# Last block's second network: rows scaled at eviction, queries and keys as rows, eleven tile places, paired scores, end in halves

## The reference

```
x   = rmsnorm(h, final_norm_w)                     # end of the first network
h   = rmsnorm(x, norm_g_2)
q, k, v, z_a, u_b, v_b, z_b, g_a, g_b = split(h @ w_in_2)   # 7 x 512, 2 x 1024 columns
y_a = stick_breaking(q, k, v) * silu(z_a)          # 8 heads of 64, causal
y_b = spatial_gating(gelu(u_b), gelu(v_b)) * silu(z_b)
out = rmsnorm(x + (sigmoid(g_a)*(y_a@w_up_a) + sigmoid(g_b)*(y_b@w_up_b)) @ w_out_2, final_norm_g_2)
```

## Time and profile before

| | us |
|---|---|
| median of 3 executions | 2019.4 |
| lowest, highest | 2016.98, 2019.96 |
| span of the profiled execution (first to last instruction) | 2014.6 |
| TensorE busy (matrix products) | 1671.1 (83%) |
| VectorE busy | 1328.1 (66%) |
| ScalarE busy | 658.9 (33%) |
| GpSimd busy | 589.6 (29%) |
| moved by DMA | 738.52 MB, mean 367 GB/s |

### The profile page before, as it was taken

The page is one execution under the profiler, slowest core; times in us unless marked ns, Lnnn a source line. Parts: engine busy times, 40 slices in busy tenths (PEclk is TensorE's granted clock), DMA queues, the critical chain, the costliest instruction groups (busy, mean ns, idle before and its releaser), DMA issues.

```text
span 2014.6 us, 20417 instructions
## 1 busy us (share of the span) xinstructions
PE 1671.1 (83%) x6878; PEld 830.8 (41%) x6878; DVE 1328.1 (66%) x3461; ACT 658.9 (33%) x1239; POOL 589.6 (29%) x516
## 2 busy tenths in 40 slices
PE   7977798678898998786589988899996877877997
PEld 7436463225454443233145434443434322222653
DVE  4227787975788888876876678966665579744231
ACT  3122433323344265221241134521221245311361
POOL 0002333432332343434433323333223334321000
PEclk9988998989999998888889999899998998899999
DMA  6438999999999998999999999999999999999665
GB/s 225 123 117 333 416 417 418 420 418 416 398 394 354 354 413 340 371 418 417 422 418 418 418 404 369 387 419 418 418 413 351 417 410 402 420 417 374 194 220 192
DMA packets 132903, 738.52 MB, mean 367 GB/s; under 512 B 15920, under 2 KB 17584, under 8 KB 67264
## 3 DMA queue, kind: packets, MB, share of 16 engines
q0 software_dynamic: 73728, 536.90, 65.4%
q1 hardware_dynamic: 59072, 200.32, 26.6%
HBM read 735.07 MB, written 2.10 MB: 366 GB/s over the span
## 4 chain that ended last, share of the span: by engine, by line
PE 41%; DMA 27%; DVE 19%; issue 5%; ACT 5%; POOL 2%; SPq 0%; DVEq 0%; POOLq 0%; ACTq 0%
PE pa L844 22%; DMA uv_rows<-in_peer_uv,small 18%; PE py L844 10%; DMA wbuf<-in_wt 9%; PE pb L844 8%; DVE uv_rows L1809 6%; ACT area L1204 2%; ACT L1198 2%; POOL uv_rows L1999 2%; DVE tk L1819 1%; DVE tk L1818 1%; DVE area L1873 1%; ACT small L1204 1%; DVE small L1796 1%; ACT an L1204 1%
## 5 line engine op out<-in xcount | busy, mean ns | idle before, releaser
L1999 POOL DMA_INDIRECT uv_rows<-in_peer_uv,small x512 | 589.4, 1151 | 1245.9 <-PE py L844 984.7
L1809 DVE CUSTOM_DVE_ANT_0 uv_rows<-uv_rows,xrep 128x1024 f32<-128x1024 f32 x512 | 615.0, 1223 | 235.0 <-DMA uv_rows<-in_peer_uv,small 231.9
L844 PE MATMUL py<-uv_rows,tk 128*64 128x512 f32 x2048 | 563.5, 677 | 212.5 <-DVE tk L1819 209.3
L844 PE MATMUL pa<-wbuf,area 128*128 128x512 f32 (+1 forms) x800 | 374.7, 609 | 25.2 <-DMA wbuf<-in_wt 22.8
L1204 ACT ACTIVATE small<-small 128x2 f32<-128x2 f32 (+4 forms) x324 | 69.2, 214 | 861.4 <-DVE small L1809 831.5
L844 PEld LDWEIGHTS py<-uv_rows,tk 128*64 128x64 f32 x2048 | 135.9, 149 | 511.7 <-DVE tk L1819 282.6
L1198 ACT ACT_TABLE_LOAD x250 | 320.8, 1283 | 5.4 <-DVE small L1905 1.0
L844 PEld LDWEIGHTS pa<-wbuf,area 128*128 128x128 f32 (+1 forms) x800 | 141.3, 188 | 242.2 <-issue 197.7
L844 PE MATMUL pa<-area,wbuf 128*128 128x128 f32 (+2 forms) x1152 | 188.4, 322 | 22.7 <-issue 11.9
L844 PEld LDWEIGHTS pa<-area,wbuf 128*128 128x128 f32 x1152 | 166.2, 198 | 60.6 <-issue 34.3
L844 PE MATMUL pb<-wbuf,area 128*128 128x512 f32 x352 | 165.5, 616 | 14.6 <-DMA wbuf<-in_wt 9.6
(11 more groups left out here) (210 smaller groups left out, 1092.2 us busy)
## 6 DMA issues: line engine op xcount, KB each, us to landing
wbuf<-in_wt SPq DMA_DIRECT2D x352, 512.0 KB
uv_rows<-in_peer_uv,small POOLq DMA_INDIRECT x512
wbuf<-in_skT SPq DMA_DIRECT2D x15, 256.0 KB
h<-in_x SPq DMA_DIRECT2D x4, 512.0 KB
out<-h SPq DMA_DIRECT2D x4, 512.0 KB, 5.6
an<-in_x SPq DMA_DIRECT2D x3, 512.0 KB
area<-in_finw SPq DMA_DIRECT2D x2, 512.0 KB, 8.0
area<-in_masks SPq DMA_DIRECT2D x1, 512.0 KB, 6.8
```

Source lines behind the costliest of these rows:

```text
L844: return nc.tensor.matmul(o, l, r, start=start, stop=stop, skip_group_check=True)
L1809: last = V.tensor_tensor_reduce(uv_rows[:, n % RING, 0:D], uv_rows[:, n % RING, 0:D], xrep[:, b % 2, n % TG, :], 1.0, 0.0, ALU.mult, ALU.a ...
L1999: nc.gpsimd.indirect_dma_start(uv_rows[:, n % RING, :], None, t["peer_uv"], bass.IndirectOffsetOnAxis(ap=expert_ids[:, c:c + 1].bitcast(U3 ...
```

## The change

It touches the last block and the scores of the first network, in these parts.

- **Scaled at eviction.** `take`, `n1`, `m1`, `n2`, `n3` of block 3 go. VectorE multiplies the expert sums by the norm weight straight out of PSUM (`last_rows_up`, step `hu`), TensorE turns the product in two halves, and the norm's second weight is applied at that eviction. ScalarE takes squares of the sums and of the products and makes from them one factor per row for both norms (`last_scales`); that factor is applied as `scale=` when ScalarE empties a bank of row results. The residual is scaled later (`hx`).
- **Queries and keys in rows.** `q2r`, `k2r` are chunks by rows, then turned (`qt`, `kt`). The values' chunk is listed between them, ahead of the pipeline.
- **Eleven places.** From the tile `TAIL` (the first of `q2r`) on, tiles go round four places of `wbuf` and seven in the gather ring's first half. A first load into the latter waits for the sum over gathers 504 to 507; the load of `TAIL` waits until the last gather has landed.
- **Paired scores.** `zp` makes two heads' scores into two B banks, products over rows 0 to 63 and 64 to 127 next to each other and then the masks; `zl` is the rest of the old `zs`. In `scores` the two parts' products are put next to each other too, with both banks taken first.
- **End in halves.** `ud` of the second half is cut in two rows. `mh` turns half of the merged rows, and `wo` runs both column halves over the first half of the contraction and then over the second (`halves_tile`). The final norm takes each half's squares as it is ready, multiplies by the weight ahead of the root, scales one half on VectorE and one on ScalarE, and stores the two halves by themselves (`last_store`, `last_products`, `last_scaled`, step `fl`).

```diff
     g = (b,)
-    rows = [[("n1", b), ("m1", b), ("n2", b), ("n3", b)], tiles("q2", g) + tiles("k2", g)]
-    fill = [tiles(name, g) for name in ("v2", "vb", "ub", "zb", "za")]
+    rows = [[("hu", b)], tiles("q2r", g), tiles("k2r", g), [("qt", b)], tiles("v2", g), [("kt", b)]]
+    fill = [tiles(name, g) for name in ("vb", "ub", "zb", "za")]
     fill += [tiles(name, g, c) for name in ("gb", "ga") for c in range(2)]
-    fill += [[("ud", g, c, i) for i in range(2)] for c in range(2)]
-    between = {2: ("ln", b), 3: ("l2", b), 4: ("sg", b), 5: ("yb", b)}
-    units = units2(g)
-    for n in range(len(units) + 3):
+    fill += [[("ud", g, 0, i) for i in range(2)], [("ud", g, 1, 0)], [("ud", g, 1, 1)]]
+    between = {0: ("hx", b), 2: ("ln", b), 3: ("l2", b), 4: ("sg", b), 5: ("yb", b)}
+    n_units = H2
+    for n in range(n_units + 3):
         row = {4: [("fin", b - 1)], 5: [("fd", b - 1), ("store", b - 1)]}.get(n, [])
         for lag, names in ((3, ("zv",)), (2, ("zt",)), (1, ("zd", "ze"))):
-            if 0 <= n - lag < len(units):
-                row += [(name, *units[n - lag]) for name in names]
+            if 0 <= n - lag < n_units:
+                row += [(name, b, n - lag) for name in names]
         if n in between:
             row.append(between[n])
-        if n < len(units):
-            row.append(("zs", *units[n]))
+        if n < n_units:
+            row += [("zp", b, n // 2)] * (n % 2 == 0) + [("zl", b, n)]
         rows.append(row + fill[n])
     rows += [[("ya", b)], [("yo", b)]] + [[("ua", g, c, i) for i in range(2)] for c in range(2)]
-    rows += [[("mt", b)], tiles("wo", g, 0), tiles("wo", g, 1), [("fin", b), ("fd", b), ("store", b)]]
-    return rows
+    for h in range(2):
+        rows += [[("mh", b, h)]] + [[("wo", g, c, 2 * h + i) for i in range(2)] for c in range(2)]
+    return rows + [[("fl", b)]]
...
 A_AT, B_AT, LOADS, FREED = ends()
+TAIL = LOADS.index(("q2r", POST[-1], 0))
+def places():
+    spots, nth, before, last, count = [], [], [], {}, {}
+    for n in range(len(LOADS)):
+        j = (n - TAIL) % (NW + XW) if n >= TAIL else 0
+        spot = j if j >= NW else (TAIL + j if n >= TAIL else n) % NW
+        spots.append(spot)
+        before.append(last.get(spot))
+        count[spot] = count.get(spot, 0) + 1
+        nth.append(count[spot])
+        last[spot] = n
+    return spots, nth, before
+SPOTS, NTH, SPOT_BEFORE = places()
+def stick_bank(b, u):
+    return B_AT[("zp", b, u // 2)] - 1 + u % 2 if b == NB - 1 else B_AT[("zs", b, u)]
...
+        p4 = Arena(ring, D + XW * TILE, RING * 2 * D)
         ub_last, zb_last, vc_last, vq_last, up_last = (p4.take(W) for _ in range(5))
         ga_last, gb_last = cut(p4.take(2 * W), 2, W), cut(p4.take(2 * W), 2, W)
         yT_last, merged_last = p4.take(KT * P), p4.take(D)
+        q_rows, k_rows = p4.take(W), p4.take(W)
...
-                if n >= NW:
-                    kind, count = FREED[n - NW]
+                if SPOT_BEFORE[n] is not None:
+                    kind, count = FREED[SPOT_BEFORE[n]]
                     sp.wait_ge({"a": a_full, "b": b_full, "w": w_done}[kind], count)
+                elif SPOTS[n] >= NW:
+                    sp.wait_ge(uv_free, GATHERS - RING + 2 * BATCH)
+                if n == TAIL:
+                    sp.wait_ge(uv_full[RING - 1], 16 * (GATHERS // RING))
                 s = LOADS[n]
...
                     sp.wait_ge(fin_ready, b + 1)
                     sp.dma_start(out[P * b:P * (b + 1), :], h1[:, b, :]).then_inc(stored, 16)
+                elif s[0] == "fl":
+                    for c in (1, 0):
+                        half = slice(W * c, W * (c + 1))
+                        sp.wait_ge(*((fin_ready, NB) if c else (half_ready, 1)))
...
                     open_banks.clear()
+            def halves_tile(src, c, i, halves):
+                w = cut(tile(), 2, W)
+                if i == 0:
+                    halves[c] = b_bank()
+                    open_banks.append(c)
+                for k in range(2):
+                    last = mm(halves[c][:, :], src[:, 2 * i + k, :], w[:, k, :], i + k == 0, i == 3 and k == 1)
+                last.then_inc(*((b_full, 1) if i == 3 else (w_done, 1)))
+                if i == 3:
+                    open_banks.remove(c)
+            def quarter_transposes(src):
+                ps = a_bank()
+                for k in range(4):
+                    last = nc.tensor.transpose(ps[:, P * k:P * (k + 1)], src[:, P * k:P * (k + 1)], ident)
+                last.then_inc(a_full, 1)
             def transposes(src, bank, full):
...
                 lo = NM if b == NB - 1 else 0
-                for part in range(2):
+                parts = [a_bank(), a_bank()]
+                for part, ps in enumerate(parts):
                     rows_ = slice(DH * part, DH * (part + 1))
-                    ps = a_bank()
                     mm(ps[:, 0:end - lo], q[rows_, hh, P * j:P * (j + 1)], kT[rows_, hh, lo:end], True, False)
+                for ps in parts:
                     mm(ps[:, end - lo - P:end - lo], ident, tri, False, True).then_inc(a_full, 1)
                 if lo:
...
+            def paired_scores(b, pair):
+                q = cut(q2_words[:, 0:4 * P], 4, P)
+                if pair == 0:
+                    pe.wait_ge(a_free, A_AT[("kt", b)])
+                banks = [b_bank(), b_bank()]
+                for part, ps in enumerate(banks):
+                    r = slice(DH2 * part, DH2 * (part + 1))
+                    mm(ps[:, :], q[r, pair, :], k2T[r, pair, :], True, False)
+                for ps in banks:
+                    mm(ps[:, W - P:], ident, stri, False, True).then_inc(b_full, 1)
...
+                    if name == "q2r" and i % 2 == 0:
+                        pe.wait_ge(b_free, B_AT[("hu", g[-1])] - 1 + i // 2)
                     rows_tile(cut(hT_words[:, 0:KT * P * len(g)], KT, P * len(g)), g, i, 4, a_bank, a_full)
+                elif name == "hu":
+                    for h in range(2):
+                        pe.wait_ge(u_ready, h + 1)
+                        ps = b_bank()
+                        for k in range(4):
+                            last = nc.tensor.transpose(ps[:, P * k:P * (k + 1)], an[:, P * (4 * h + k):P * (4 * h + k + 1)], ident)
+                        last.then_inc(b_full, 1)
+                elif name in ("qt", "kt"):
+                    pe.wait_ge(a_free, A_AT[("q2r" if name == "qt" else "k2r", POST[-1], 3)])
+                    quarter_transposes(q_rows if name == "qt" else k_rows)
+                elif name == "zp":
...
-                    pe.wait_ge(b_free, B_AT[("ua" if is_last(g) else "ud", g, 1, 1)])
-                    transposes(merged_last if is_last(g) else merged[:, index2(s[1]), :], a_bank, a_full)
+                    pe.wait_ge(b_free, B_AT[("ud", g, 1, 1)])
+                    transposes(merged[:, index2(s[1]), :], a_bank, a_full)
+                elif name == "mh":
+                    b, h = s[1:]
+                    pe.wait_ge(b_free, B_AT[("ua", POST_OF[b], h, 1)])
+                    quarter_transposes(merged_last[:, W * h:W * (h + 1)])
+                elif name == "wo" and is_last(s[1]):
+                    g, c, i = s[1:]
+                    if c == 0 and i % 2 == 0:
+                        pe.wait_ge(a_free, A_AT[("mh", g[-1], i // 2)])
+                    halves_tile(cut(hT_words[:, 0:KT * P], KT, P), c, i, halves)
...
             def empty(dst, src, func=ACT.Copy, scale=1.0):
                 fn(dst, src, func, scale=scale).then_inc(a_free, 1)
+            def last_scales(b):
+                act.wait_ge(uv_free, gather_y(b))
+                for c in (1, 0):
+                    if c == 0:
+                        act.wait_ge(u_ready, 1)
+                    last = fn(yT_last[:, W * c:W * (c + 1)], psum_y[c][:, :], ACT.Square, accum_out=last_ss[:, 2 * c:2 * c + 1])
+                    if c == 1:
+                        last.then_inc(y1_read, 1)
+                for c in range(2):
+                    act.wait_ge(u_ready, c + 1)
+                    last = fn(merged_last[:, W * c:W * (c + 1)], an[:, W * c:W * (c + 1)], ACT.Square,
+                              accum_out=last_ss[:, 2 * c + 1:2 * c + 2])
+                last.then_inc(sq_done, 1)
+                act.wait_ge(ss_ready, 1)
+                step(fn(last_ln, last_tot[:, 0:1], ACT.Ln, scale=1.0 / D, bias=eps))
+                fn(last_half, last_ln, ACT.Copy, scale=-0.5)
+                fn(last_r1, last_ln, ACT.Exp, scale=-0.5)
+                step(fn(last_r1s, last_ln, ACT.Exp, scale=-1.0, bias=neg_ln_d))
+                step(fn(last_ln2, last_tot[:, 1:2], ACT.Ln, scale=last_r1s, bias=eps))
+                step(fn(last_s, last_ln2, ACT.Exp, scale=-0.5, bias=last_half))
+                fn(last_s8, last_s, ACT.Copy, scale=DH2 ** -0.5).then_inc(scales, 1)
+                act.wait_ge(scales, 1)
+            def last_store(b):
+                tables(ACT.Exp)
+                for c in range(2):
```

(59 more changed lines are left out.)

62 lines of the change are left out of this document (45 added, 17 removed).

## The result

The changed kernel takes 2002.47 us (median of 4, 2001.65 to 2003.2), the kernel before 2019.43 beside it (2016.98 to 2019.96): ratio 0.9928, 95% interval 0.9909 to 0.9948, 17.0 us faster. The forecast was 1999.5 with 1993 to 2007: right in direction and range, 3.0 us too low.

A forecast was written before the change was run, and what follows sets the result against it. Transfers were taken to bound the kernel until the last gather lands, then TensorE in the last block's second network, alone for 155.5 us. Gains of 19.85 us off the 2014.6 span, plus 4.8 around it, gave 1999.5 us, range 1993 to 2007.

The forecast's parts named there:

- Loads: Before the last gather lands: holding back the tail's tiles stops 1.26 tiles going ahead of gathers, gain 1.6 us.
- To the first query product: From the last weighted sum to the first query product: 2.4 us in place of 10.25, gain 7.85 us.
- Queries and keys: Last block's query and key products made in row chunks: 15.5 us in place of 17.68, gain 2.2 us.
- Paired scores: Last second network's scores: two heads run at the same time, 1.69 us a pair, gain 5.0 us.
- rival 1: Paired scores: the two products do not overlap, so the kernel takes 2003.4 us; chance 0.17.
- Output product in halves: From the up product's end to the output product's end: 16.3 us in place of 17.59, gain 1.3 us.
- Final steps: From the output product's end to the span's end: about 6.0 us in place of 6.9, gain 0.9 us.
- Scores of the first network: Opening heads: products side by side with both banks taken first, gain 1.0 us; later blocks' heads taken as nothing.
- 2: Start of the query and key chunks: TensorE's clock is low again, costing 1.9 us, 2001.4 us; chance 0.08.
- 3: Tail's tiles: eleven loads in flight land together, late, losing 7.6 us, 2007.1 us; chance 0.07.
- 4: First network: taking two banks first delays weighted sums and gathers, up to 2038.4 us; chance 0.02 slower.
- 5: First network's scores in block 3: its heads gain 4 us more, 1995.5 us; chance 0.05.

The follow-up runs named there:

- the waiting kernel: Changed kernel with the first query product waiting until ScalarE has made the last row factor: 2005.15 us, ratio 0.9918.
- order alone: Changed kernel with only the order of the last second network's steps changed: 1997.95 us, ratio 0.9903; again 1998.25 us, ratio 0.9881.

## Why the prediction was right, point by point

- **Loads (1.6, measured 0).** The step that failed is the price, "worth 0.66 MB / 413 GB/s = 1.6 us". That some 1.3 tiles moved ahead of the last landing fits the rows (0.7 to 1.5 in the run without the wait), but they were priced as if every byte pushed back one of a gather. The last gather leaves room (109 GB/s where nothing else is issued), and from the dot product of gather 508 to that of 511 it is 11.17 us without the wait and 11.12 to 11.16 with it.
- **To the first query product (7.85, measured 7.95).** 10.25 to 2.3. Right, and so was the cover: the factors are ready at 1866.13 and the first eviction with them starts at 1870.66, 5.0 and 9.5 us after the sum (forecast: 6 and 9.3).
- **Queries and keys (2.2, measured 2.0).** 22.57 less 6.88 of the values is 15.7. The exposed eviction is 1.2 us and not 0.85: the keys' eviction stands in line behind the values'. As the prediction said, the gain hangs on the clock: with it low, 17.4 us are left of 17.7.
- **Paired scores (5.0, measured 4.9).** Four times 1.70 to 1.77 in place of eight 1.47; apart 2.94 to 3.01. The estimate drawn from column neighbours carried over to row neighbours. Apart they cost more than the 2.55 that rival 1 had. The Trainium skill, TensorEngine Tiling (Array Packing), section Tiling Modes, has row tiles run in parallel; by the 1.13 us for four passes this trace agrees.
- **Output product in halves (1.3, measured 1.1).** The halves cost about what was summed (16.5 against 16.3), but they are not the cause of the gain: in one piece it is 1.6. Gating and turning the first half ahead of the second gives it, and the cut takes 0.5 back.
- **Final steps (0.9, measured 1.2).** TensorE's end to the span's end went from 6.9 to 5.7.
- **Scores of the first network (1.0, measured nothing that shows).** The step that failed is "three of four heads wait for no bank": that held for the banks taken one at a time, but with both taken first three of the four heads of the opening wait (0.45, 0.33 and 1.83 us). In block 3, priced at nothing, three heads wait 2.55 to 3.99 us, but the run without the pairs is no faster.
- **Around the span (4.8, measured 1.8).** It was added to a span that was itself 3 us short of the median, so the two errors cancel, and the forecast stands as the median less the gain.

The forecast's gain was 19.85; 17.0 came. Of the 2.9 between, 2.6 are the loads and the scores of the first network, the two terms that lie ahead of the last sum. The balance of medians fits that: 17.0, 15.1 and 19.4 us gained in all in the three comparisons (mean 17.1), 17.1 in the tail; with a spread of 4 us between comparisons it could not show 1 us ahead of the sum. The row factors, the pairs, the wait ahead of the tail's loads, the places and the halves were each undone in a run; the queries in rows and the final steps are only read from the chain. Of the rivals, 1 fell (pairs apart), 2 came not at the chunks but at the up product, now and then and in both kernels, 3 fell (the first query product starts right behind its eviction, with no wait for a tile). Of 4 and 5 nothing shows: the last gather's dot product starts anywhere from 1851.57 to 1860.30 in the changed kernel and its variants, and neither a loss nor a gain of block 3's heads of 1 or 2 us could be told from that.

## What to carry to other kernels

Price a saving by where it lies: here all that was forecast in the part where one engine worked alone came within 0.3 us a term, and what was forecast for a stage bound by transfers or by another engine's evictions came to nothing that shows. Where a step between a sum and a product only scales rows, apply it at the eviction behind the product; the pause saved is worth its clock too. Before cutting a product in halves, look whether one neighbouring piece of work, put between the turning and the use, hides the same eviction: order alone took 4.7 us more from the tail.

## What the runs showed of the hardware

- The granted clock after a 3 us pause with four transposes in it is not fixed: of the 11 traces that have the pause the up product takes 8.83 to 8.85 us in 4 (a mean clock of 0.81) and 7.13 to 7.15 in the others. Behind the 5 us of the waiting kernel, with eight transposes in them, it was 0.54 for 3.7 us.
- Two products on the lower and upper 64 rows cost one (1.13 us for four passes of 512 columns); what a pair costs beside its passes stays at about 0.4 us (1.70 less 0.86 and 0.43).
- The last gather of 1 MB was 22.52 us under way, and over its last 2.1 us the engines moved 109 GB/s; 0.4 to 0.8 MB more of tiles in the last 4 us did not make a last gather later.
- Runs of the same kernel before spread from 2011 to 2025 us. The tails of the changed kernel agree to 0.1 us once the 1.7 us of the low clock are taken off, the two of the kernel before to 0.4 (155.5 and 155.1; only the first has a wait for a tile ahead of the keys, 0.7 us). So the spread arises ahead of the last sum; what makes it was not found.
